# Decoder layer with a mixture of experts on one core: in the last phase, roots with scale and bias, two tiles scaled by ScalarE and GpSimd

## What is computed

```python
y = y.at[slot_tok].add(yb * slot_gate[:, None])     # experts, weighed by gates
x = x + hierarchical_moe(rms_norm(x, norm_ffn), ...)

def rms_norm(x, gain):
    x32 = x.astype(jnp.float32)
    y = x32 * lax.rsqrt(jnp.mean(x32 * x32, axis=-1, keepdims=True) + NORM_EPS)
    return (y * gain.astype(jnp.float32)).astype(x.dtype)

return (rms_norm(yp, norm_final), rms_norm(ys, norm_final), ...)
```

## Time and profile before

| | us |
|---|---|
| median of 3 runs | 1843.63 |
| lowest, highest run | 1841.56, 1843.66 |
| the profiled execution | 1842.43 |
| its span | 1840.8 |
| TensorE busy in the span | 1767.7 (96%) |
| VectorE, ScalarE, GpSimd busy | 1150.5, 863.2, 481.1 |
| last phase, from the first load's issue at 1803.27 to the end | 37.5 |

### The profile page before, as it was taken

How to read it: one execution, slowest core, us unless ns; L and a number is a source line. 1 busy time by engine, 2 the same in 40 slices (tenths; PEclk the granted TensorE clock), 3 DMA queues, 4 the chain that set the end, 5 groups by cost and what they waited for, 6 DMA issues and landing times. The chain is left out here.

```text
span 1840.8 us, 28440 instructions
## 1 busy us (share of the span) xinstructions
PE 1767.7 (96%) x9908; PEld 1525.4 (83%) x9908; DVE 1150.5 (62%) x1952; ACT 863.2 (47%) x1554; POOL 481.1 (26%) x496
## 2 busy tenths in 40 slices
PE   7989999999999999999999999959999999999997
PEld 6878888999999788888878978748888888888882
DVE  5267665311111354545456546679999999999985
ACT  5255555311111223332223223348877788777872
POOL 3022332000000232323231112223765333333320
PEclk9999999999999999999999999979999999999998
DMA  7121211332213203030204643279999999999987
GB/s 223 56 51 43 55 47 47 93 93 69 77 51 90 69 27 92 23 94 23 94 1 133 199 132 125 85 282 376 392 388 387 389 382 388 382 385 393 381 336 288
DMA packets 149420, 333.18 MB, mean 181 GB/s; under 512 B 33728, under 2 KB 102896, under 8 KB 123680
## 3 DMA queue, kind: packets, MB, share of 16 engines
q1 hardware_dynamic: 127264, 278.06, 41.6%
q0 software_dynamic: 21408, 53.27, 8.4%
q10 hardware_dynamic: 672, 0.85, 0.3%
HBM read 304.11 MB, written 46.35 MB: 190 GB/s over the span
## 5 line engine op out<-in xcount | busy, mean ns | idle before, releaser
L2826 POOL DMA_INDIRECT y_d<-e_y,e_idxs x32 | 138.8, 4336 | 208.0 <-DVE e_y L2930 193.5
L2901 DVE TENSOR_TENSOR e_Lg<-e_rawg,e_Hg 128x1024 fp32r<-128x1024 f32 x128 | 148.2, 1219 | 8.1 <-ACT e_Hg L2850 8.1
L2901 DVE TENSOR_TENSOR e_Lu<-e_rawu,e_Hu 128x1024 fp32r<-128x1024 f32 x128 | 147.8, 1213 | 0.0
L2901 DVE TENSOR_TENSOR e_Ld<-e_rawd,e_Hd 128x1024 fp32r<-128x1024 f32 x124 | 143.1, 1213 | 0.0
L2850 ACT ACTIVATE e_Hg<-e_rawg 128x1024 fp32r<-128x1024 f32 x128 | 124.8, 1051 | 9.0 <-DMA e_rawg<-in_w_gate 9.0
L2850 ACT ACTIVATE e_Hu<-e_rawu 128x1024 fp32r<-128x1024 f32 x124 | 120.9, 1059 | 0.0
L2850 ACT ACTIVATE e_Hd<-e_rawd 128x1024 fp32r<-128x1024 f32 x124 | 120.8, 1051 | 0.0
L162 PE MATMUL bank<-r_wH,xH 128*128 128x512 f32 x256 | 106.1, 414 | 3.7 <-DVE r_gs L1510 3.2
L162 PE MATMUL bank<-e_Hg,e_xH 128*128 128x512 f32 x256 | 100.8, 394 | 3.4 <-DVE e_xL L2907 3.4
L162 PE MATMUL bank<-e_Hu,e_xH 128*128 128x512 f32 x256 | 102.8, 402 | 0.0
L164 PE MATMUL bank<-r_wH,xL 128*128 128x512 f32 x256 | 101.3, 396 | 0.0
(11 more groups left out here) (464 smaller groups left out, 4763.5 us busy)
## 6 DMA issues: line engine op xcount, KB each, us to landing
e_rawg<-in_w_gate SPq DMA_DIRECT2D x64, 1024.0 KB, 8.5
e_rawu<-in_w_up SPq DMA_DIRECT2D x64, 1024.0 KB, 7.3
e_rawd<-in_w_down SPq DMA_DIRECT2D x62, 1024.0 KB, 8.0
raw<-in_w_in SPq DMA_DIRECT2D x51, 512.0 KB, 4.0
c_Y<-y_d SPq DMA_DIRECT2D x8, 1024.0 KB, 13.5
m_t<-b_m_s POOLq DMA_DIRECT2D x8, 528.0 KB, 3.4
m_gate<-gate_t POOLq DMA_DIRECT2D x8, 528.0 KB, 3.9
m_m<-m_t POOLq DMA_DIRECT2D x8, 528.0 KB, 3.9
```

The source lines that it names most:

```text
L2826: pool.indirect_dma_start(out=ch.y_d, out_offset=bass.IndirectOffsetOnAxis(ap=idx[:, e % IDX, 1:2], axis=0), in_=y[:], in_offset=None, bou ...
L2901: dve.tensor_tensor(L[kind][:, q], raw[kind][:, q], H[kind][:, q].bitcast(F32), ALU.subtract).then_inc(w_lo[kind], 1)
```

## The change

The epsilon is kept in a tile of one column, `eps`, which VectorE fills. The root is taken from the sum of squares itself, with scale 1/1024 and bias `eps`, and VectorE's mean step goes away; `mean` now only adds the two halves of a tile on TensorE. For tiles 2 and 4 (`ON_POOL`) VectorE computes only the reciprocal. ScalarE scales the tile with it by a copy (`shrink`), called after the root of the tile that follows, and GpSimd multiplies with the gain and counts `gained`. The store of such a tile waits for `gained` instead of `o_done`.

```diff
+    ON_POOL = (2, 4)
@@ sync
-            sp.wait_ge(self.o_done, n + 1)
+            if t in self.ON_POOL:
+                sp.wait_ge(self.gained, self.ON_POOL.index(t) + 1)
+            else:
+                sp.wait_ge(self.o_done, n + 1 - sum(u in self.ON_POOL for u in self.ORDER[:n]))
@@
+    def gpsimd(self, pool):
+        for i, t in enumerate(self.ON_POOL):
+            pool.wait_ge(self.shrunk, i + 1)
+            pool.tensor_tensor(self.Y[:, t, 0], self.Y[:, t, 0], self.gain[:], ALU.mult).then_inc(self.gained, 1)
@@ scalar
+        def shrink(t):
+            act.wait_ge(self.rstd_done, order.index(t) + 1)
+            act.activation(self.Y[:, t, 0], self.Y[:, t, 1], ACT.Copy, scale=stat[:, t, 3:4]).then_inc(self.shrunk, 1)
@@ root
-            act.wait_ge(self.ms_done, n + 1)
-            act.activation(stat[0:m, t, 2:3], stat[0:m, t, 1:2], ACT.Sqrt).then_inc(self.root_done, 1)
+            if t in self.ON_PE:
+                act.wait_ge(self.ms_part, pe_tiles.index(t) + 1)
+            else:
+                act.wait_ge(self.sq_done, n + 1)
+            act.activation(stat[0:m, t, 2:3], stat[0:m, t, 0:1], ACT.Sqrt, bias=self.eps[0:m], scale=1.0 / D).then_inc(self.root_done, 1)
@@
+        act.wait_ge(self.eps_set, 1)
         square(0)
-        for t in range(NT):
-            if t + 1 < NT:
-                square(t + 1)
-            root(t)
+        for n in range(NT):
+            if n + 1 < NT:
+                square(n + 1)
+            root(n)
+            if n and order[n - 1] in self.ON_POOL:
+                shrink(order[n - 1])
@@ vector, mean
-            dve.wait_ge(self.sq_done, n + 1)
             if t in self.ON_PE:
+                dve.wait_ge(self.sq_done, n + 1)
                 dve.tensor_tensor(stat[0:m, t, 0:1], stat[0:m, t, 0:1], stat[0:m, t, 4:5], ALU.add).then_inc(self.ms_part, 1)
-                dve.wait_ge(self.ms_part, pe_tiles.index(t) + 1)
-            dve.tensor_scalar(stat[0:m, t, 1:2], stat[0:m, t, 0:1], 1.0 / D, EPS, ALU.mult, ALU.add).then_inc(self.ms_done, 1)
@@ scale
             dve.reciprocal(stat[0:m, t, 3:4], stat[0:m, t, 2:3]).then_inc(self.rstd_done, 1)
+            if t in self.ON_POOL:
+                return
@@
+        dve.memset(self.eps[:], EPS).then_inc(self.eps_set, 1)
@@ stage_experts, gpsimd
+                pool.wait_ge(combine.g_in, 16)
+                combine.gpsimd(pool)
```

More of the change, by code:

```diff
@@ L2596, in __init__ @@
         self.ch, self.gain, self.served = ch, gain, served
-        self.g_in, self.y_in, self.half, self.a_done, self.sq_done, self.ms_part, self.ms_done, self.root_done, self.rstd_done, self.o_done, self.o_st = (
-            ch.sem("c_gain"), [ch.sem(f"c_y{t}") for t in range(NT)], ch.sem("c_half"), ch.sem("c_a"), ch.sem("c_sq"), ch.sem("c_part"), ch.sem("c_ms"),
+        self.g_in, self.y_in, self.half, self.a_done, self.sq_done, self.ms_part, self.root_done, self.rstd_done, self.o_done, self.o_st = (
+            ch.sem("c_gain"), [ch.sem(f"c_y{t}") for t in range(NT)], ch.sem("c_half"), ch.sem("c_a"), ch.sem("c_sq"), ch.sem("c_part"),
             ch.sem("c_root"), ch.sem("c_rstd"), ch.sem("c_o"), ch.sem("c_st"))
         self.diag_done, self.pe_done = ch.sem("c_diag"), ch.sem("c_pe")
-        self.table = ch.sem("c_table")
+        self.table, self.shrunk, self.gained, self.eps_set = ch.sem("c_table"), ch.sem("c_shrunk"), ch.sem("c_gained"), ch.sem("c_eps_set")
         self.Y = sb("c_Y", [P, NT, 2, D])
         self.junk, self.stat = sb("c_junk", [P, D]), sb("c_stat", [P, NT, 5])
+        self.eps = sb("c_eps", [P, 1])
     def place_diag(self, sb):
```

## The result

The changed kernel takes 1847.44 us (median of 6 runs, 1845.09 to 1849.89), the kernel before 1842.85 us (6 runs, 1840.18 to 1844.37). The ratio is 1.0028 with a 95% interval of 1.0018 to 1.0037: **slower by 0.28%**. The forecast was 0.10%, on the near side of the 0.2% that counts as a difference.

What follows compares the result with a forecast made beforehand. TensorE until 1831.62, then ScalarE and VectorE steps and the last store set the end; (1) gains 0.25 us, but tile 4's late copy and backed-up stores make it 1.9 us more: 1845.5 us, range 1842.6 to 1847.8.

Steps and rivals of the forecast that it cites:

- (4b): GpSimd and SyncE's store queue: tile 4's late product holds back three stores; last landing 1842.3, span 1842.7, 1.9 us more.
- the line of 3.7: Whole kernel: about 0.2% (3.7 us) is what a measurement can tell from no change.
- slow tail in the store queue: Stores at the end: a backed-up queue can add some 1.5 us, counted into the top of the range.
- (1): Mean and epsilon folded into the root: nine VectorE instructions go, gaining 0.25 us at the end.
- (2): One memset of epsilon and one wait for it, before the first tile is loaded: no effect.
- (3): Tile 2 off VectorE: the 1.28 us product stood before 1832.9, where VectorE waits for TensorE; no gain at the end.
- (4a): ScalarE's queue: tile 4's copy delays the last roots, so VectorE ends 0.35 us later instead of 0.25 us earlier.
- The hold: GpSimd and VectorE may hinder each other: beside a GpSimd product a VectorE sum took 0.85 us, 0.16 at best.
- A: Rival at the store queue: it doesn't back up, only (4a) counts, +0.35 us, 1844.0 us; chance 0.14.
- B: Rival: copy and store of tile 4 don't matter, the 0.25 us of (1) remain, 1843.4 us; chance 0.11.
- C: Rival: GpSimd's product of tile 4 waits for VectorE's products, +6.0 us, 1849.6 us; chance 0.08 with other stretching of tile 4's path.

Runs made afterwards that it cites:

- the late memset with and without a drain: Kernel before plus a one-column GpSimd memset behind the last tile's product: 1847.38 us, ratio 1.0019; with a GpSimd drain at the phase's start too: 1842.12 us, 0.9994.
- tile 4's early product: Changed kernel with an early GpSimd drain and tile 4's copy called ahead of the square of tile 6: 1842.13 us, ratio 0.9998.

## Why the prediction was wrong

**The step that failed is the last one of (4b)**: "Span 1842.3 + 0.4". The 0.4 us were read off the kernel before as what lies between the last landing and the end. That held there only because every engine but SyncE had reported: the last of their drains, VectorE's, was over at 1837.8. GpSimd's drain behind its new last product was put at nothing, without a reason; it took 9.36 us. The forecast's own sum has GpSimd work until 1835.9, so such a drain outlasts the last landing at 1842.3. A row with 9.3 us for it was in the trace of the kernel before. It gives 1835.9 + 9.4 + 0.2 = 1845.5 in the terms of the forecast, 4.7 us more and over the line of 3.7. The drain added to the changed kernel, and the late memset with and without a drain, show this cause by itself.

**Luck in the range.** The median of 1847.44 lies under the range's top of 1847.8, but that top was made of a slow tail in the store queue and of scatter, not of what happened. The forecast gave "slower" a chance of 0.09, and without the 2.6 us of the drain its line of 3.7 us would not have been passed. (The 0.8 us of scatter in the range was small, too: the three runs behind it lie 2.1 us apart.)

**(1) Roots**: the mechanism and the sign were right; 0.1 to 0.2 us measured instead of 0.25. The root with bias takes 0.29 us instead of the assumed 0.20, inside the bounds, and the reciprocal of tile 5 starts 0.04 us behind it: in front of tile 5's product 0.07 us are gained, where the forecast had 0.15 to 0.19.

**(2)** Nothing, as forecast.

**(3) Tile 2**: nothing at the end in the changed kernel, as forecast: the sum for tile 6 starts 1.30 us after the square of tile 6, before and now. The reason given was too short, though: with tile 2 alone it costs 0.9 us through the held sum. In the full change this hid, since tile 4's product had left VectorE too.

**(4a) ScalarE's queue**: right. VectorE's end moved by 0.6 us against the 0.35 forecast, since two roots on the path are 0.09 us longer each and the copy took 1.14 for 1.05 us. So VectorE waited 0.65 us for the root of tile 6, where the forecast had 0.43.

**(4b) Store queue**: right in kind, 2.1 us there. The term that was mis-sized is the product, 2.35 for 1.90 us; the store of tile 4 went out 4.94 us after the square of tile 6, by the forecast 4.30 (the other 0.2 us are the root and the copy). The pace behind it was 1.3 us, the forecast 1.2 to 1.25.

**The hold** between GpSimd and VectorE: held were instructions with two tensor inputs in SBUF, the sum of tile 5 (1.64 us instead of 0.15) and, in other kernels here, a weighing (2.07 us instead of 1.26, 3.47 instead of 1.28). The forecast's sum lets VectorE's products of tiles 5 and 6 run beside GpSimd's product of tile 4, and no row of the kernel before shows that; in the changed kernel they do, with 1.41 us each, as alone. Why the one kind is held and the other is not, no run shows.

**Rivals.** A and B left the queue out and fell with it. C named another mechanism for the slow side and is refuted: the products started 0.46 us (tile 2) and 0.08 us (tile 4) after their copies ended, the latter beside VectorE's product of tile 5, which reads PSUM. But the prediction's argument against C, that in the trace of before it was VectorE that waited, was too narrow. In the same trace, in the mixer, GpSimd waited too. Its sum of 128x128 at line 1371 takes 0.46 us, but 1.50 us in the six cases in which a VectorE instruction with both inputs in SBUF starts 0.04 us ahead of it, and there VectorE takes no longer than alone:

```profile
636.74 0.46 POOL L1371 TENSOR_TENSOR r_rotd<-r_ta,r_tb 128x128 f32<-128x128 f32 x1
...
644.34 1.23 DVE L1506 TENSOR_TENSOR r_wL<-raw,r_wH 128x1024 fp32r<-128x1024 f32 x1 [0.51 <-ACT r_wH L1403]
644.38 1.50 POOL L1371 TENSOR_TENSOR r_rotd<-r_ta,r_tb 128x128 f32<-128x128 f32 x1
```

So each of the two engines is seen to wait for the other; but beside VectorE's products of tiles 5 and 6, which read PSUM, tile 4's product took 2.35 us, as tile 2's did (2.34). The slow side came, but by a path that no rival had.

## What to carry to other kernels

Work added to an engine that had long finished can lengthen the end of a program even if its own duration is hidden. Here tile 4's product of 2.35 us was over at 1834.78, the 9.36 us of drain behind it at 1844.14, and the span at 1844.3; with tile 2 alone on GpSimd the drain was over at 1838.7 of 1840.8, and hidden. So ask what that engine still has to do after its last instruction, and look at the line where all engines meet. A drain placed in GpSimd's idle time took the whole 2.6 us of it off the end here, for one line. And before the engine that a row names as the last is believed, compare the drains of all engines on that line with the end of the span.

## What the runs showed of the hardware

- GpSimd's drain took 9.3 to 9.4 us at the start of the last phase in every kernel that had it there, and as much when it came 25 to 32 us later, so it does not run down by itself while GpSimd idles. After one drain the next took 0.10 us beyond the product. Earlier in the kernel before it took less: 5.7 us at the end of a block in which GpSimd had issued 44 DMAs (the issue of the last, 0.53 us, included), 1.2 us after 10 (with a copy of 0.30 us), and 0.1 us beyond a product in a block without any. In the last block GpSimd issues over 150. In these four blocks the drain is longer where more DMAs went before, but no run varied their number, and the blocks also differ in kind and size of the DMAs and in all else that GpSimd did.

```profile
L3128 POOLq DRAIN  x1: 5712/5712/5712, 1059.7 to 1059.7; - x1
```

```profile
L249 POOLq DRAIN  x1: 1222/1222/1222, 75.4 to 75.4; - x1
```

```profile
L604 POOLq DRAIN  x1: 2003/2003/2003, 313.4 to 313.4; - x1
```

- GpSimd's first product started 0.46 us after the end of its copy in the four kernels without an added drain (1826.09 after 1825.63 in the changed one), and 0.08 to 0.09 us after it in the four with one. Why, no run shows.

- Starts 0.04 us apart don't tell who is held. Beside tile 4's early product VectorE was, though its row starts first (1828.35 against 1828.39). In the six cases of the mixer GpSimd was, with VectorE's row first by the same 0.04 us (644.34 against 644.38). What decides it, no row shows.
- ScalarE's copy with a column as scale took 1.13 to 1.15 us, the plain one of the same size 1.05; its root with bias and scale 0.29 us, without 0.20.
